# Prompt attention and routing first, and the prompt's expert rows between the sample's attention maps and its lead-in

## What is computed

```python
def trunk_layer(x, cvec, p, layer, ctx, rope):
    sh1, sc1, gt1, sh2, sc2, gt2 = modulation(cvec, p['w_mod'], p['b_mod'])
    h = rms_norm(x, p['g_norm1']) * (1 + sc1) + sh1
    mix, ctx_out = token_mixers(h, p, layer, ctx, rope)   
    x = x + gt1 * mix
    h = rms_norm(x, p['g_norm2']) * (1 + sc2) + sh2
    x = x + gt2 * peer_ffn(h, p['w_pq'], p['peer_keys'], p['peer_u'], p['peer_v'])
```

## Time and profile before

| | us |
|---|---|
| runs before, median of 3 (lowest, highest) | 5220.91 (5215.0, 5221.15) |
| span of the profiled execution | 5217.8 |
| time of that execution outside its span | 3.1, as far as the median tells |
| attention and lead-in, layer 1 and 2 | 301 and 297 |
| from the first gather to the last dot, layer 1 and 2 | 1668 and 1665 |

### The profile page before, as it was taken

How to read it: one execution, slowest core, us unless ns; L and a number is a source line. 1 busy time by engine, 2 the same in 40 slices (tenths; PEclk the granted TensorE clock), 3 DMA queues, 4 the chain that set the end, 5 groups by cost and what they waited for, 6 DMA issues and landing times. The chain is left out here.

```text
span 5217.8 us, 51329 instructions
## 1 busy us (share of the span) xinstructions
PE 4403.5 (84%) x14836; PEld 2229.8 (43%) x14836; DVE 3444.6 (66%) x9196; ACT 1436.0 (28%) x4114; POOL 1498.3 (29%) x1410
## 2 busy tenths in 40 slices
PE   7999898888878878887788998988988788897776
PEld 3588665433323323322235886654333233332222
DVE  5555565667676777777565555746677767777775
ACT  2211342222222222222222113522222222222222
POOL 0122100333343434433301220004333334344432
PEclk9988899999999999999999888999999999999999
DMA  7100102899999999999870001019999999999997
GB/s 258 39 3 1 48 1 73 365 418 415 406 416 405 414 420 401 415 419 415 344 258 17 3 1 48 1 73 416 420 414 411 420 404 414 410 405 420 420 414 311
DMA packets 243939, 1481.06 MB, mean 284 GB/s; under 512 B 26384, under 2 KB 32144, under 8 KB 79296
## 3 DMA queue, kind: packets, MB, share of 16 engines
q0 software_dynamic: 184320, 1342.26, 62.5%
q1 hardware_dynamic: 59264, 135.37, 7.2%
q10 hardware_dynamic: 64, 0.07, 0.0%
HBM read 1473.96 MB, written 3.64 MB: 283 GB/s over the span
## 5 line engine op out<-in xcount | busy, mean ns | idle before, releaser
L1646 PE MATMUL psall<-left,diag 128*128 128x512 f32 x2848 | 1373.0, 613 | 323.3 <-ACT diag L1541 322.8
L1646 PE MATMUL psall<-right,diag 128*128 128x512 f32 x2272 | 1105.0, 617 | 265.7 <-ACT diag L1541 265.6
L1379 POOL DMA_INDIRECT left<-in_peer_uv,eidx x712 | 735.8, 1033 | 1797.3 <-PE psall L1646 1058.3
L1464 DVE CUSTOM_DVE_ANT_0 left<-left,mixed 128x1024 f32<-128x1024 f32 x712 | 873.2, 1226 | 543.1 <-DMA left<-in_peer_uv,eidx 543.1
L1646 PEld LDWEIGHTS psall<-left,diag 128*128 128x128 f32 x2848 | 500.1, 190 | 1163.8 <-ACT diag L1541 721.2
L1464 DVE CUSTOM_DVE_ANT_0 right<-right,mixed 128x1024 f32<-128x1024 f32 x568 | 696.8, 1227 | 422.3 <-DMA right<-in_peer_uv,eidx 422.3
L1548 ACT ACTIVATE act<-dot 128x1 f32<-128x1 f32 x1280 | 259.5, 203 | 2411.7 <-DVE dot L1464 2410.7
L1379 POOL DMA_INDIRECT right<-in_peer_uv,eidx x568 | 587.4, 1034 | 884.8 <-PE psall L1646 861.5
L1646 PEld LDWEIGHTS psall<-right,diag 128*128 128x128 f32 x2272 | 401.2, 191 | 945.3 <-ACT diag L1541 597.6
L1541 ACT ACTIVATE diag<-cons,wgt 128x128 f32<-128x128 f32 x1280 | 493.8, 386 | 2.3 <-issue 0.3
L498 POOL TENSOR_TENSOR mlt<-lt,lmask 128x512 f32<-128x512 f32 x120 | 173.0, 1452 | 535.6 <-DVE lt L596 370.8
(11 more groups left out here) (289 smaller groups left out, 5106.5 us busy)
## 6 DMA issues: line engine op xcount, KB each, us to landing
wlate<-in_w_mod SPq DMA_DIRECT2D x32, 1024.0 KB, 5.3
wq<-in_w_pq SPq DMA_DIRECT2D x64, 512.0 KB, 7.9
left<-in_peer_uv,eidx POOLq DMA_INDIRECT x712, 15.9
right<-in_peer_uv,eidx POOLq DMA_INDIRECT x568, 15.9
w<-in_w_mod SPq DMA_DIRECT2D x4, 2048.0 KB, 10.8
wtm<-in_w_mod SPq DMA_DIRECT2D x4, 2048.0 KB, 18.0
wtm<-in_w_in_tm SPq DMA_DIRECT2D x4, 2048.0 KB, 9.0
right<-in_w_out SPq DMA_DIRECT2D x4, 2048.0 KB, 11.4
```

Source lines behind the costliest of these rows:

```text
L1379: nc.gpsimd.indirect_dma_start(out=p.slots[n % SLOT], out_offset=None, in_=d["peer_uv"], in_offset=bass.IndirectOffsetOnAxis(ap=p.eidx[:, ...
L1464: nc.vector.tensor_tensor_reduce(out=u_row, in0=u_row, in1=p.mixed[:, t, :], scale=1.0, scalar=0.0, op0=ALU.mult, op1=ALU.add, accum_out=p ...
L1646: mm = nc.tensor.matmul(bank, p.diag[:, n % DIAGS, :], p.slots[n % SLOT][:, D + 512 * c:D + 512 * c + 512], start=(s == 0), stop=(s == UNI ...
```

## The change

`attend` and `tail` become one block, `mix_and_feed`. All prompt maps (m = 0 to 15) come first, then the 64 sample maps (16 to 79). Between sample maps 16 to 40 each engine gets the prompt's output projection, norm, queries, scores and first two routing items. From m = 40 on, DVE handles one of the prompt's 128 rows per map, 45 of them up to m = 84; PE handles one row less at each step. The other 83 rows stand between the sample's projections (two rows after every half projection), turnings (two), half queries (three) and key scores (three). These rows turn over five slots; the sample's 512 rows then use ten.

To keep one table on ACT, the prompt's gelu is written with Tanh and four more 128x1 operations on DVE (`cubic`, `gated_weight`), and both square roots become `rsqrt`, 15 linked operations on DVE. There are two score banks instead of three. Maps of kind b are no longer scaled on DVE; their sums are, on the way out, and come out with tokens on partitions, so that all eight blocks of a tile are turned before the projection, not four. The output weights (4 MB) and the keys are loaded twice a layer, for the sample after its last map. DIAGS goes from 8 to 5, SUBS from 5 to 4. The sample's own ring keeps its instructions.

```diff
-SLOT = 9
-DIAGS = 8
+PROWS = C * 2 * TOPK
+RING_P = 5
+S_ORDER = (3, 4, 0, 1, 2, 5, 6, 7, 8, 9)
+SLOT = 10
+DIAGS = 5
...
+PM = 16
+PB = 45
...
+def rows_by(m):
+
+    return min(max(m - (PM + 23), 0), PB)
...
+def rsqrt(p, own, y, x, n, scale):
...
+    own.link(v.tensor_scalar(val, x, scale, EPS, ALU.mult, ALU.add))
+    own.link(v.tensor_scalar(seed, val.bitcast(U32), 1, None, ALU.logical_shift_right))
+    own.link(v.tensor_scalar(y.bitcast(U32), seed, -1.0, float(0x5F3759DF), ALU.mult, ALU.add))
+    for _ in range(4):
+        own.link(v.tensor_tensor(half, y, y, ALU.mult))
+        own.link(v.scalar_tensor_tensor(out=half, in0=half, scalar=-0.5, in1=val, op0=ALU.mult, op1=ALU.mult))
+        own.link(v.scalar_tensor_tensor(out=y, in0=half, scalar=1.5, in1=y, op0=ALU.add, op1=ALU.mult))
...
+def slot_of(n):
+
+    return n % RING_P if n < PROWS else S_ORDER[(n - PROWS) % len(S_ORDER)]
...
+    groups = [("b", 2 * g, "a", g, "b", 2 * g + 1, t) for t in range(NT) for g in range(HA)]
...
+    def score_cols(m, nk):
+
+        a = 1024 * (m % 2)
+        return p.psall[:, a:a + nk]
...
+            for c in range(2):
+                load_wout(c, p.woutP[:, c, :, :])
...
+            sp.wait_ge(sem("wout_mm"), 2)
+            for i in range(4 * C):
+                load_wq(i, p.wqP)
+                if i == WR - 1:
+                    load_keys(p.keysP[:, :])
...
+            sp.wait_ge(sem("a_out"), len(outs))
+            spread(p.gt1[1], d["mid_rows"][0][1:2, :], "load_gt1")
+            for c in range(2):
+                load_wout(c, p.woutS[:, c, :, :])
+            spread(p.sc2[1], d["mid_rows"][2][1:2, :], "load_sc2")
+            spread(p.g2row[1], d["g_norm2"][bass.ds(lay, 1)], "load_sc2")
+            spread(p.sh2[1], d["mid_rows"][1][1:2, :], "load_sh2")
+            for i in range(4 * C, 8 * C):
+                load_wq(i, p.wqS)
...
+                if n == 0:
+                    pool.wait_ge(sem("sc_mm"), C)
+                if n == PROWS + RING_P:
+                    pool.wait_ge(sem("res1"), 2 * NT)
+                if previous[n] >= 0:
+                    pool.wait_ge(sem("row_free"), previous[n] + 1)
...
+                if kind == "b":
+                    own.link(nc.vector.reciprocal(r0, p.esum[:, m % 4:m % 4 + 1]))
+                    return
...
+                    nc.vector.tensor_scalar(p.mixed[:, t, W_A + h * 64:W_A + h * 64 + 64], sums_of(o), p.r01[:, o % 4, 0:1], None,
+                                            ALU.mult).then_inc(sem("a_out"), 1)
...
+                rsqrt(p, own, p.ra[:, 0:4], p.ssa[:, t, :], 4, 1.0 / 64)
...
-            residual(0)
-            norm(0)
...
-            dve.wait_ge(sem("h2_ready"), NT)
-            pieces(1, 0, TOPK)
...
+
+                x, q, z = (a[:, n % 16:n % 16 + 1] for a in (p.dot, p.gq, p.gz))
+                own.link(nc.vector.scalar_tensor_tensor(out=q, in0=x, scalar=0.044715, in1=x, op0=ALU.mult, op1=ALU.mult))
+                nc.vector.scalar_tensor_tensor(out=z, in0=q, scalar=1.0, in1=x, op0=ALU.add, op1=ALU.mult).then_inc(sem("dots"), 1)
...
+                own.link(nc.vector.scalar_tensor_tensor(out=q, in0=y, scalar=1.0, in1=x, op0=ALU.add, op1=ALU.mult))
+                nc.vector.scalar_tensor_tensor(out=p.wgt[:, n % 16:n % 16 + 1], in0=q, scalar=0.5, in1=p.gat[:, t, col:col + 1],
+                                               op0=ALU.mult, op1=ALU.mult).then_inc(sem("weights"), 1)
...
+            def rows_to(end):
+
+                for n in range(done[0], min(end, PROWS)):
+                    own.link(dot(n))
+                    cubic(n)
+                    if n >= 1:
+                        gated_weight(n - 1)
+                    k, s = divmod(n, TOPK)
+                    if k + AHEAD < 2 * C:
+                        top_piece(p, top, s, k + AHEAD)
...
+            for m in range(len(maps) + FLUSH):
+                if m < len(maps):
+                    max_of(m)
+                if m - 3 in out_after:
+                    out(out_after[m - 3][0])
+                if m in out_after:
+                    weigh_map(out_after[m][0])
+                if m == PM + 3:
+                    subnorm(0)
+                    gain(0)
+                if m == PM + 8:
...
+                for k in range(2):
+                    if PM + 17 + 4 * k <= m < PM + 21 + 4 * k:
+                        pieces(k, 4 * (m - PM - 17 - 4 * k), 4 * (m - PM - 16 - 4 * k))
+                rows_to(rows_by(m))
+
+            for t in range(1, NT):
+                subnorm(t)
+                rows_to(PB + 2 * t)
+            gain(1)
+            for t in range(1, NT):
+                rows_to(PB + 8 * t)
+                residual(t, 0)
+                residual(t, 1)
+                norm(t)
+            rows_to(PB + 66)
+            for i in range(TOPK):
+                pieces(2 * C, i, i + 1)
+                rows_to(PB + 67 + i)
+            rows_to(PROWS)
+            gated_weight(PROWS - 1)
+            pieces(2 * C + 1, 0, TOPK)
...
+                    nc.scalar.activation(p.act2[:, n % 16:n % 16 + 1], p.gz[:, n % 16:n % 16 + 1], ACT.Tanh,
+                                         scale=GELU).then_inc(sem("gelus"), 1)
+                    if n >= 1:
+                        diag_of(n - 1)
+                    k, s = divmod(n, TOPK)
...
+                if m >= 2:
+                    pe.wait_ge(sem("a_exp"), m - 1)
...
+                for n in range(done[0], min(end, PROWS)):
+                    if n == 0:
+                        pe.wait_ge(sem("sub_in"), C)
+                    pe.wait_ge(sem("diags"), n + 1)
+                    for c in range(2):
+                        mm = nc.tensor.matmul(ps[6 + c], p.diag[:, n % DIAGS, :], p.slots[slot_of(n)][:, D + 512 * c:D + 512 * c + 512],
+                                              start=(n == 0), stop=(n == PROWS - 1))
+                    mm.then_inc(sem("row_free"), 1)
...
+            for m in range(len(maps) + FLUSH):
+                if m < len(maps):
+                    scores(m)
+                if m - 3 in out_after:
+                    sums(out_after[m - 3][0])
+                if m - 2 in out_after:
+                    turn_map(out_after[m - 2][0])
...
+                for c in range(C):
+                    if m == PM + 13 + 2 * c:
+                        query(4 * c)
+                        query(4 * c + 1)
+                    if m == PM + 14 + 2 * c:
...
+
+            for t in range(1, NT):
+                turn_mixed(t)
+                for j in range(4):
+                    project(t, j // 2, j % 2)
+                    rows_to(PB + 8 * (t - 1) + 2 * j + 1)
+            for t in range(1, NT):
+                turn(t)
+                rows_to(PB + 31 + 2 * t)
+            for i in range(4):
+                for half in range(2):
+                    query(4 * C + i, half)
+                    rows_to(PB + 39 + 6 * i + 3 * half + 3)
+            for t in range(1, NT):
+                score_unit(unit(0, t))
+                rows_to(PB + 63 + 3 * t)
+            rows_to(PROWS)
```

More of the change, by code:

```diff
@@ L1385, in _ @@
             own, top = Chain(dve, sem("dve_out")), Chain(dve, sem("piece"))
-            before = [dve.snap(lay * (16 * uses)) for uses in (-(-ROWS // SLOT), ROWS // SLOT)]
-            dve.wait_ge(sem("load_sc2"), 48)
-            for g in range(2):
-                nc.vector.scalar_tensor_tensor(out=p.rows[:, 1, g, :], in0=p.rows[:, 1, g, :], scalar=1.0, in1=p.g2row,
+            before = {k: dve.snap(lay * (16 * k)) for k in sorted(set(uses))}
+            dve.wait_ge(sem("lam_exp"), 1)
+            own.link(nc.vector.tensor_tensor(p.lam[:, 4:5], p.lam[:, 3:4], p.lam[:, 2:3], ALU.subtract))
@@ L1401, in norm @@
[L1401 to L1410 removed]
+                                                        in1=p.sc2[g], op0=ALU.mult, op1=ALU.mult))
@@ new lines, in norm, with residual @@
+                nc.vector.tensor_tensor(p.mixed[:, t, :], p.mixed[:, t, :], p.sh2[g], ALU.add).then_inc(sem("h2_ready"), 1)
+            def residual(t, c):
+                g = min(t, 1)
+                j = 2 * t + c
+                cols = slice(c * 512, c * 512 + 512)
+                dve.wait_ge(sem("wout_mm"), j + 1)
+                own.link(nc.vector.tensor_tensor(p.gated[g][:, cols], ps[6 + j] if t == 0 else ps[2 + j % 4], p.gt1[g][:, cols], ALU.mult))
+                nc.vector.tensor_tensor(p.x[:, t, cols], p.x[:, t, cols], p.gated[g][:, cols], ALU.add).then_inc(sem("res1"), 1)
@@ L1432, in _, with dot @@
-            pieces(1, 0, TOPK)
+            def dot(n):
+                t, _ = place(n)
+                dve.wait_ge(sem(f"row_in{slot_of(n)}"), before[uses[slot_of(n)]] + 16 * arrived[n])
+                u_row = p.slots[slot_of(n)][:, 0:D]
+                return nc.vector.tensor_tensor_reduce(out=u_row, in0=u_row, in1=p.mixed[:, t, :], scale=1.0,
+                                                      scalar=0.0, op0=ALU.mult, op1=ALU.add,
```

(33 more changed lines are left out.)

894 lines of the change are left out of this document (439 added, 455 removed).

## The result

The changed kernel takes 5706.51 us (5682.09 to 5708.05, four runs), against 5217.95 before: a ratio of 1.093 (95% interval 1.0915 to 1.0946), 489 us more. Forecast were 372 more, 5593, in a range of 5430 to 5800. The profiled execution has a span of 5702.7 us, against 5217.8.

What follows compares the result with a forecast made beforehand. Bound: row transfers in the ring, PE in the maps. Attention and lead-in 26 + 125 + 302 + 30 + 16 + 316 = 815 us a layer, against 299, less 330 saved; 5217.8 + 372 + 3.1 = 5593, range 5430 to 5800.

Steps and rivals of the forecast that it cites:

- The chain PE, VectorE, ScalarE, PE: Maps 40 to 79: each row's weight waits for its map's maximum, next scores for the row; 7.5 us a map.
- The clock: Maps 40 to 79: waits sometimes drop PE to 1.2 GHz; a quarter of 112, so 30 us a layer.
- The loop: Maps 40 to 79 with a row each: 40 x 7.5 = 302 us a layer, plus 30 for lower PE speed.
- the ring: Sample's 512 rows stay bound by transfers; 128 of 640 rows leave, saving 330 us a layer.
- rival 1: Maps 40 to 79: PE stays at its lower speed, 102 us a layer more, 5797 us; chance 0.12.
- The forecast's own bounds: Map loop 6.6 to 8.4 us a map, row period 2.6 to 3.6, clock 0 to 80; together 5430 to 5720.
- Maps 16 to 39: These sample maps with the prompt's projection, norms and queries: 63 + 48 us on PE, 14 for norms; 125 a layer.
- the flush: Five steps behind the last map that finish its work: 16 us a layer.
- The sample's lead-in: Behind the last map, with 83 prompt rows: 51, 102, 109 and 54 us for its parts, together 316 a layer.
- The slot relation: Prompt rows among turnings and queries: 4T = L + 4.75, period T, landing time L, five slots; T taken as 3.2 us.
- Rival 2: Prompt rows behind the maps: five slots starve, T = 5.2, 102 us a layer more, about 5800; chance 0.05.
- Rival 3: Maps and lead-in: row work fills idle time, 4.44 us a map, 45 us a layer less, about 5130; chance 0.08.

Runs made afterwards that it cites:

- The kernel with one step of lag: Changed kernel with TensorE taking its prompt row one step later in the maps; 5257.72 us, 1.0099 of before.
- the kernel with the filler: Changed kernel with two unneeded matmuls ahead of each row in the maps; 5546.54 us, 1.0636 of before.
- the kernel with a filler in the prompt maps: One step of lag and ten slots for the last 45 prompt rows, plus an unread matmul behind each of the last eight prompt maps; 5219.3 us.

## Why the prediction was right in kind and 117 us short

**Direction and mechanism.** The chain PE, VectorE, ScalarE, PE is in the timeline link for link, and its length at the full clock was forecast at 7.54; 7.69 was measured with the clock at 0.94. The kernel with one step of lag shows that the order alone made it.

**The clock, the term that was mis-sized.** "I take about a quarter of the price, 30 us" should have been most of it. The loop took 398 us for 302 + 30; by the kernel with the filler 90 of the 96 above 302 are the clock, and 6 a chain of 7.69 instead of 7.54. 60 us a layer too little are 120 over two layers, as much as the whole miss. The two ends were known, 0.99 in the ring at waits of 0.5 to 1.5 us and 0.50 after an idle PE; the loop's waits of 2.0 to 3.9 us, which the text had worked out, lie beyond the ring's, and I put them nearer to the ring. The argument against rival 1, that a slow PE is busy longer and so brings the clock back, holds only for moments: the granted clock is 0.57 from 1100 to 1116 us, 1.00 from 1116 to 1121 and 0.66 from 1121 to 1126, and TensorE is still idle for 2.81 us of the 10.08 us step above. The Trainium skill, TensorE: Matmul & The Clock Gate, section "Why this matters for your kernels", says that gaps between bursts of matmuls bring the slower level back. The trace agrees, 0.62 with the gaps and 0.94 with the filler in them; how short a gap does it, no run here settles. Rival 1 was right in the loop, and the measured time lies nearer to its 5797 (91 us) than to the forecast's 5593 (114). Its 5797 was too high since it took the whole 112, added 20 us in prompt maps and first rows, and counted 20 too little for the ring.

The forecast's own bounds for the clock, 0 to 80 us a layer, do not hold the 90. That the time lies inside 5720 all the same, where the bounds taken together end, owes something to luck: without the 20 us a layer that the ring gave back beyond the forecast it would be some 5745.

**Maps 16 to 39, 11 us over, and the flush, 6 over.** The 125 were counted at the full clock; the window has 0.81, and the kernel with a filler in the prompt maps got 5.5 us back with the clock at 0.88. Here, too, the clock was left out; what makes the other half was not tested. In the flush the chain goes on: from the maximum of map 79 to the 46th dot the changed kernel takes 36.5 us, the one with a step of lag 24.4, and only 5.5 of the 12 are the step of map 79 itself.

**The sample's lead-in, 314.8 and 318.9 for 316.** Its parts fit as well as the sum: cut at dots 54, 78 and 112 of layer 1 they are 55, 97, 114 and 50 us, for 51, 102, 109 and 54. The slot relation that gave T = 3.2 gets the step from five slots to four right and is 0.3 us low at both. A single gather lands in 5.3 us at the least now, less than the 6.1 of the earlier trace rows. The Trainium skill, DMA: Bandwidth & Descriptors, section "Anatomy of one DMA", from which I estimated 4.4 us, is still below the trace.

**The ring, 20 less than forecast.** Cut at the sample's first gather, the DMA engines moved 411 GB/s in both (the 417 that one expectation names does not come out of these windows). 128 gathers of 1.049 MB are 134 MB, 327 us at that rate. The query weights account for the rest: 24 loads of 0.52 MB in the stretch before and 8 in the one after, 8.4 MB and 20 us less. The forecast named them, and its 330 counts 11 us for them above the row's spacing of 2.49; together they give 347, measured are 349.5 and 346.8.

**Rivals 2 and 3.** Rival 2 (slots starve at a gather of 15.9 us) is out: they land in 7.4. Rival 3's break-even, 629 us of attention and lead-in, is 649 with the 350 us that the ring gave back in layer 1. With its lag by a step really there, and ten slots, attention and lead-in take 652 us (first score at 627.84, the sample's first gather at 1280.23), and the kernel ties with the one before. So what lay between the forecast and rival 3 was one index in one line, and the slots.
